# Starting TensorE's operands at one place within 512 bytes: three small tensors moved behind the arena, views rounded up

## The reference

```python
def swiglu(x, w_gate_up, w_down):
    g, u = jnp.split(x @ w_gate_up, 2, axis=-1)
    return (jax.nn.silu(g) * u) @ w_down
...
    for e in range(N_EXPERTS):
        out = out + combine[:, e:e + 1] * swiglu(xf, w_gate_up[e], w_down[e])
```

## Time and profile before

| | |
|---|---|
| median of three runs | 2189.68 us |
| span of the profiled execution | 2188.4 us |
| TensorE busy | 2150.1 us (98%), 10935 matmuls |
| LDWEIGHTS busy | 1812.1 us (83%) |
| VectorE busy | 1592.3 us (73%) |
| ScalarE busy | 1331.8 us (61%) |
| DMA | 569.70 MB, mean 260 GB/s |

### The profile page before, as it was taken

How to read it: one execution, slowest core, us unless ns; L and a number is a source line. 1 busy time by engine, 2 the same in 40 slices (tenths; PEclk the granted TensorE clock), 3 DMA queues, 4 the chain that set the end, 5 groups by cost and what they waited for, 6 DMA issues and landing times.

```text
span 2188.4 us, 27831 instructions
## 1 busy us (share of the span) xinstructions
PE 2150.1 (98%) x10935; PEld 1812.1 (83%) x10935; DVE 1592.3 (73%) x1339; ACT 1331.8 (61%) x1151; POOL 78.0 (4%) x67
## 2 busy tenths in 40 slices
PE   7999999999998999999999999999999999999998
PEld 6988788888787888888888888888888898899987
DVE  5576555466766888888888888888896667565665
ACT  4475544455656677776777777777675555456542
POOL 3100000000000000000000000000110000000000
PEclk9999999999998999999999999999999999999999
DMA  8554565554538999999999999999996534455442
GB/s 279 156 191 147 208 201 177 183 183 155 198 139 310 335 383 375 370 375 372 386 364 381 375 377 365 382 375 370 384 374 225 173 117 153 157 178 173 134 154 77
DMA packets 249166, 569.70 MB, mean 260 GB/s; under 512 B 12169, under 2 KB 14353, under 8 KB 248817
## 3 DMA queue, kind: packets, MB, share of 16 engines
q1 hardware_dynamic: 242368, 546.41, 69.8%
q0 software_dynamic: 5136, 16.70, 2.3%
q10 hardware_dynamic: 1568, 5.31, 0.6%
HBM read 562.60 MB, written 5.78 MB: 260 GB/s over the span
## 4 chain that ended last, share of the span: by engine, by line
PE 90%; DVE 4%; DMA 3%; ACT 2%; issue 0%; SPq 0%; DVEq 0%; ACTq 0%
PE bank L908 32%; PE bank L1169 9%; PE bank L1170 9%; PE bank L1173 9%; PE bank L914 9%; PE bank L1217 5%; PE bank L1210 5%; PE bank L1212 5%; PE bank L955 3%; DMA ring<-w_in 2%; DVE halves_r L2185 1%; DMA ring<-moe_w_down 1%; ACT halves_r L1663 1%; DVE w_low L2613 0%; DMA ring<-w_out 0%
## 5 line engine op out<-in xcount | busy, mean ns | idle before, releaser
L2613 DVE TENSOR_TENSOR w_low<-ring,w_high 128x4096 fp32r<-128x4096 f32 x167 | 736.3, 4421 | 75.8 <-ACT w_high L1892 75.1
L1892 ACT ACTIVATE w_high<-ring 128x4096 fp32r<-128x4096 f32 x167 | 606.8, 3634 | 236.5 <-DMA ring<-moe_w_gate_up 141.4
L908 PE MATMUL bank<-halves_r,xT_high 128*128 128x512 f32 (+1 forms) x1856 | 563.3, 381 | 6.1 <-ACT halves_r L1663 3.1
L2185 DVE TENSOR_TENSOR halves_r<-ring,halves_r 128x2048 fp32r<-128x2048 f32 x175 | 391.6, 2265 | 162.2 <-ACT halves_r L1663 160.0
L908 PEld LDWEIGHTS bank<-halves_r,xT_high 128*128 128x128 f32 x1856 | 344.1, 189 | 73.8 <-issue 5.2
L1663 ACT ACTIVATE halves_r<-ring 128x2048 fp32r<-128x2048 f32 x175 | 326.2, 1891 | 118.7 <-DMA ring<-w_in 55.5
L1169 PE MATMUL bank<-w_high,xg_high 128*128 128x512 f32 x896 | 357.6, 399 | 1.7 <-DVE xg_low L2590 1.7
L1170 PE MATMUL bank<-w_high,xg_low 128*128 128x512 f32 x896 | 351.8, 393 | 0.0
L908 PE MATMUL bank<-halves_r,xT_low 128*128 128x512 f32 (+1 forms) x928 | 348.7, 380 | 0.0
L1173 PE MATMUL bank<-w_low,xg_high 128*128 128x512 f32 x896 | 224.3, 392 | 0.0
L908 PEld LDWEIGHTS bank<-halves_r,xT_low 128*128 128x128 f32 x928 | 175.3, 189 | 32.1
(11 more groups left out here) (392 smaller groups left out, 2312.7 us busy)
## 6 DMA issues: line engine op xcount, KB each, us to landing
ring<-moe_w_gate_up SPq DMA_DIRECT2D x224, 1024.0 KB, 10.4
ring<-moe_w_down SPq DMA_DIRECT2D x112, 1024.0 KB, 9.8
ring<-w_in SPq DMA_DIRECT2D x108, 1024.0 KB, 5.2
ring<-w_out SPq DMA_DIRECT2D x24, 1024.0 KB, 4.9
ring<-ffn_w_gate_up SPq DMA_DIRECT2D x22, 1024.0 KB, 5.3
ring<-ffn_w_down SPq DMA_DIRECT2D x11, 1024.0 KB, 4.8
ring<-w_mem_kv SPq DMA_DIRECT2D x8, 1024.0 KB, 5.1
ring<-w_branch_attn SPq DMA_DIRECT2D x4, 1024.0 KB, 5.1
```

The costliest lines, as they stand in the source:

```text
L908: return pe.matmul(o[:, a:a + n], x[:, c, b * P:(b + 1) * P], w[:, k, col:col + n], **flags)
L1892: act.activation(high_slot(k), ring[:, ring_r.slot(names[k]), :], ACT.Copy).then_inc(w_high_in[r], 1)
L2185: dve.tensor_tensor(raw_view(half, halves_r), raw_view(half), top_view(half).bitcast(F32), ALU.subtract).then_inc(raw_low_in, 1)
L2613: dve.tensor_tensor(w_low[:, slot, :], ring[:, slot, :], high_slot(k).bitcast(F32), ALU.subtract).then_inc(w_low_in[r], 1)
```

## The change

`ssq`, `rstd` and `par_all` are allocated behind `arena` in place of ahead of it, so that `arena` begins at place 0. A new method `line_up` of `Views` rounds the next view up to a whole 128 words (512 bytes). It is called in place of `A(4)` behind `zT`, and behind `par` and `xbc` in plan `C`. No instruction is added, removed or moved; only addresses differ. All views at places 192, 224 and 64 named above come to place 0.

```diff
@@ -419,17 +419,22 @@
         xT_high = rounded("xT_high", [KC, SEQ], xT_at)
         consts = sb("consts", [P, 7, P])
         ident, flip, le, lt, ge, ones, slots_row = (consts[:, k, :] for k in range(7))
+        ARENA = 25400
+        arena, arena_at = placed("arena", [P, ARENA])
         ssq = sb("ssq", [P, 8])
         rstd = sb("rstd", [P, 8])
         par_all = sb("par_all", [P, LAYERS, 80])
-        ARENA = 25400
-        arena, arena_at = placed("arena", [P, ARENA])
+        assert ring_at % (4 * P) == xT_at % (4 * P) == arena_at % (4 * P)
...
+            def line_up(self):
+
+                self.at = -(-self.at // P) * P
...
@@ -502,7 +507,7 @@
         zT = A(2, SEQ + 2)
-        A(4)
+        A.line_up()
         q_n = A(TB, ATTN)
...
@@ -573,6 +578,7 @@
         par = C(96)
+        C.line_up()
         post_row = C(D)
...
```

## The result

The changed kernel takes 2178.53 us, the median of five runs (2177.25 to 2184.32). The kernel before, five runs with it: 2189.95 us (2189.39 to 2192.78). The ratio is 0.9945, with a 95% interval from 0.9933 to 0.9957: faster by 0.43 to 0.67%. The forecast was 2177.2, with a range from 2171.7 to 2183.8; by the medians the gain is 11.4 us, where 12.5 were forecast from the kernel before.

A forecast was written before the change was run, and what follows sets the result against it. The prediction took TensorE's matmul start distances as the bound, with DMA nearly a second. Experts' 10.0 us (11.2 less 1.2 given back) plus 2.5 dense made 12.5 us off 2189.7, so 2177.2 us, range 2171.7 to 2183.8.

The forecast's parts named there:

- The bound: Whole kernel: TensorE busy 98% of the span, time being to a tenth the matmul count times the distance between starts.
- The reference level: Layer 0 feed-forward, both operands at place 0: 96 matmuls of 512 columns in 21.81 us, 227.2 ns each.
- the row that didn't fit: Expert line 1173: both operands at 0 yet 230.0 ns, put down to following 16 matmuls with unequal places.
- Gate and up tiles, down tiles: Experts' matmuls at 227.4 ns: 1.2 us an expert from gate and up, 0.2 from down, 11.2 us in all.
- The DMA: Expert loads: can speed up by at least 1.6 us in experts 0 to 6; last expert gives back 1.2 us.
- the rival in which the DMA binds: Experts keep their 120.3 us since rests between loads can't be used; only dense 2.5 us gained, 2187.2 us; chance 6%.
- Dense stages: Matmuls outside the experts: gains less a 0.4 us loss at 256 columns give 3.0 us, counted as 2.5.
- the 60-matmul pieces: Dense stages, gate tile (48) plus branch tile (12): 13.88 or 13.69 us to 13.64, 1.8 us for 12 pieces.
- Everything else at nothing: VectorE, ScalarE and DMA: same bytes in the same order at other addresses, place costing nothing within 1%.
- The partial rival: Up tiles go no lower than line 1173's 230.0 ns; 6.9 us less in all, 2182.8 us; chance 13%.
- Placement does nothing: Rival: matmul differences come from tensors and traffic, not place; no gain, 2189.7 us; chance 7%.
- Equal places collide: Rival: expert and dense matmuls each pay 2.1 ns more, as at 256 columns; 10.5 us slower, 2200.2 us; chance 4%.

The follow-up runs named there:

- the probes: Changed kernel with groups of 24 matmuls added at its very end, other engines idle, operand distances or widths varied; 5.44 us for 24 at distance 0, 512 columns.
- the arena at 128: Changed kernel with 128 bytes put between consts and arena; 2196.02 us, ratio 1.0025 to the kernel before.
- the small gathers: Changed kernel with the last expert's four gathers cut from 4096 to 256 bytes a row; last expert 117.7 us against 119.2, span 2175.4 us against 2175.1.
- the first probe: Changed kernel with 42 groups of 24 matmuls added at its end, stationary operand 0 to 480 bytes off; 512 columns: 227.1 ns at 256 bytes, 229.6 at 192.

## Why the prediction was right

*The bound.* TensorE's start distances set the time, and its busy share did not show it. The 14.1 us less of busy time for 13.3 us of span confirm it.

*The reference level.* 227 ns for 512 columns at equal places, at 0 as at 192: shown by the probes (5.44 us for 24 at 0, 5.45 with both at 192) and by the whole of the changed kernel. Line 1173, the row that didn't fit, was rightly read: with equal places ahead of it, it takes 1.82 us for eight; with the arena at 128 its own places are equal and those ahead of it are not, and its eight take 1.85 us.

*Gate and up tiles, down tiles.* 1.4 us an expert were forecast and 1.3 measured (120.3 to 119.0). One term was misread: the restart behind the transposes is 3.80 - 3.69 = 0.11 us by the earlier trace rows, not 0.08, and it didn't fall (3.76 against 3.62 us after the change).

*The DMA.* Experts 0 to 6 got all of their gain, so the rival in which the DMA binds fell. But the rest that I took for the slack gave little of it: it is 1.5 us in place of 1.6. The DMA's mean rate over the third expert went from 375 to 379 GB/s. In the last expert 1.2 of 1.4 us were to be given back; it went from 119.8 to 119.2 us, so about 0.7 of 1.3 were. The mechanism is shown by the small gathers. Experts in all: 10.0 us forecast, 9.9 measured. That they agree so well is luck in part: the first seven gave 9.3 us and not 9.8, the last one 0.6 and not 0.2.

*Dense stages.* 3.0 us were summed and 2.5 counted; the traces show 3.5, of which 0.6 are the start's and 0.8 the low clock's, so 2.1 are left for the places. Within it one term was mis-sized: the 60-matmul pieces shown went from 13.88 to 13.82 and from 13.69 to 13.65 us, and the eight that stand whole in the chain fell by 0.07 us on average and not 0.15, so 0.8 us for twelve and not 1.8. I had set the whole excess over 227.4 ns down to place; most of it stayed with equal places. In the piece at 155.70 us of the changed kernel the first start, behind small matmuls, is 338 ns ahead of the second, the next four distances are 228 to 236 ns, and nearly all others 226 or 227. So what stayed is the restart. `hidT` (0.42 us), the memory products (0.15 for 24) and the loss at 256 columns (2.0 ns each) came as said. Two pieces of 84 matmuls with `yd` tiles, which the sum left out, gave 0.19 us (19.25 to 19.06) and 0.18 (19.26 to 19.08).

*Everything else at nothing* held: VectorE's subtractions of 4096 columns take 4421 ns on average as before, ScalarE's roundings 3636 against 3634.

*The total.* The runs list 2177.25 us with a span of 2175.1, so some 2.2 us lie outside the span. The 1.3 us of the prediction compared the span of one execution with the time of others; the forecast, a median less a gain, doesn't hang on it. Of the bounds, the upper one comes to 2184.0 us by its own terms (5.6 - 2.4 + 2.5 = 5.7 us less), not 2183.8.

*The partial rival* fell: the up tiles went to 227 ns, not to 230. *Placement does nothing* fell with the probe. The rule of the Trainium skill that I set beside it ("TensorE: Matmul & The Clock Gate", "Step-by-step: what each phase is for"), that the next load takes nothing from the running matmul, doesn't agree with these runs at 512 columns, where the place of the next stationary operand is worth 4 to 7 ns in 227; at 384 columns nothing here speaks against it. *Equal places collide* fell for 512 columns. At 256, where it was read, equal places are among the dearest, but 160 bytes are as dear.

*The step that the document carried over untested* was the 512 bytes of the change. The period is 256.

## What to carry to other kernels

Where TensorE is the bound and its matmuls run back to back, divide the pieces of the chain by their counts and compare equal shapes: 3% between 227 and 234 ns don't show in any duration or busy share, and tensors of a few hundred bytes ahead of a large one can decide it. With 512 moving columns of `float32r` and 128 stationary ones, start stationary and moving operands at the same place within 256 bytes; with other widths measure first, as 384 columns didn't care and 256 took least at 8 bytes (115.4 ns against 120 at equal places). Before a gain is counted, look for the stretch where another stream has no rest, and for what stands behind it: a gain there can end as a wait. And before a difference of a microsecond is set down to a change, compare the granted clock of the same stretch in both traces.

## What was not expected of the hardware

- The period of 256 bytes: 24 matmuls take 5.59, 5.60 and 5.51 us at 32, 64 and 192 bytes, and the same at 288, 320 and 448.
- 384 columns take 173.3 ns at every distance tried (0, 32 and 192 bytes), and fewer stationary columns make 512-column matmuls slower, 230.4 ns at 64 against 226.7 at 128.
- After another distance, a stream takes several matmuls to find its rhythm: eight in line 1557 of the first probe, 5.48 us for 24 in place of 5.44.
- The granted clock doesn't fall at one place of the program. After TensorE's idle 2.3 us at the end of the experts it fell to 0.50 less than 1 us behind their end in the changed kernel; with small gathers it stayed 1.00 for 5 us behind the same idle time and fell after a second one of 2.1 us.
